# Prompt masks added on VectorE in one operation with the queries' factor and the maximum, probabilities weighed on VectorE head by head

## What is computed

```python
# DSA: the indexer scores keys, the best k_sel are kept, softmax over these
score = einsum('qh,qhs->qs', wi, relu(einsum('qhd,sd->qhs', qi, ki) * D_IDX ** -0.5))
_, sel = top_k(where(key_pos <= pos, score, -inf), k_sel)        # 64 of 256 for the prompt
logits = einsum('qngd,qknd->qngk', qa, ka[sel]) * HEAD_DIM ** -0.5
p = softmax(where(sel <= pos, logits, -inf));  oA = einsum('qngk,qknd->qngd', p, va[sel])
# MoBA: the block of 256 keys that holds the query, causal
p = softmax(where(causal, qb . kb * HEAD_DIM ** -0.5, -inf));    oB = p . vb
x += (sigmoid(gA) * (oA @ w_up_a) + sigmoid(gB) * (oB @ w_up_b)) @ w_out
```

## Time and profile before

| | us |
|---|---|
| runs, median of 3 (lowest, highest) | 639.16 (638.4, 639.34) |
| the profiled execution | 638.18 |
| its span, first to last instruction | 636.6 |
| PE busy | 628.3 (99%) |
| VectorE busy | 408.9 (64%) |
| ScalarE busy | 298.7 (47%) |
| POOL busy | 154.6 (24%) |

### The profile page before, as it was taken

How to read it: one execution, slowest core, us unless ns; L and a number is a source line. 1 busy time by engine, 2 the same in 40 slices (tenths; PEclk the granted TensorE clock), 3 DMA queues, 4 the chain that set the end, 5 groups by cost and what they waited for, 6 DMA issues and landing times.

```text
span 636.6 us, 13030 instructions
## 1 busy us (share of the span) xinstructions
PE 628.3 (99%) x4822; PEld 608.7 (96%) x4822; DVE 408.9 (64%) x671; ACT 298.7 (47%) x480; POOL 154.6 (24%) x211
## 2 busy tenths in 40 slices
PE   8999999999999999999899999999999999999998
PEld 6999999999999999889789899999999999999998
DVE  5765656565555568599888739867565656574441
ACT  7644444444343355545554657454434444443330
POOL 1477776000011216466603100260000000000000
PEclk9999999999999999999999999999999999999999
DMA  8777676535554556633232314545555554555530
GB/s 323 273 223 241 198 241 200 188 129 184 177 164 153 186 157 202 204 125 121 70 132 72 128 68 154 178 132 167 164 158 173 150 180 150 172 153 196 173 106 20
DMA packets 34907, 104.79 MB, mean 165 GB/s; under 512 B 6065, under 2 KB 8753, under 8 KB 34865
## 3 DMA queue, kind: packets, MB, share of 16 engines
q1 hardware_dynamic: 30432, 97.98, 46.6%
q0 software_dynamic: 3616, 4.73, 2.6%
q10 hardware_dynamic: 816, 1.51, 0.6%
HBM read 100.21 MB, written 1.70 MB: 160 GB/s over the span
## 4 chain that ended last, share of the span: by engine, by line
PE 86%; DVE 3%; DMA 2%; POOL 2%; SPq 2%; ACT 2%; issue 1%; ACTq 0%; POOLq 0%
PE ps L1189 27%; PE ps L1191 26%; PE ps L1190 26%; SPq L486 1%; DVE wlo L862 1%; PE ps L1321 1%; DMA x<-in_x 1%; PE ps L1394 1%; PE ps L1353 1%; PE ps L1384 1%; PE ps L1305 1%; ACT whi L627 1%; PE ps L1213 0%; DVE tmp L1102 0%; DMA kv<-kv 0%
## 5 line engine op out<-in xcount | busy, mean ns | idle before, releaser
L862 DVE TENSOR_TENSOR wlo<-raw,whi 128x1024 fp32r<-128x1024 f32 (+2 forms) x180 | 220.2, 1227 | 124.3 <-ACT whi L627 123.9
L1189 PE MATMUL ps<-nhi,whi 128*128 128x288 f32 (+1 forms) x944 | 283.4, 300 | 0.4 <-DVE kv L1092 0.2
L1190 PE MATMUL ps<-nlo,whi 128*128 128x288 f32 (+1 forms) x944 | 278.6, 295 | 0.0
L1191 PE MATMUL ps<-nhi,wlo 128*128 128x288 f32 (+1 forms) x944 | 277.7, 294 | 0.0
L627 ACT ACTIVATE whi<-raw 128x1024 fp32r<-128x1024 f32 (+2 forms) x180 | 181.3, 1030 | 126.9 <-PE ps L1191 114.1
L1189 PEld LDWEIGHTS ps<-nhi,whi 128*128 128x128 f32 (+1 forms) x944 | 176.5, 187 | 5.4 <-issue 3.0
L1191 PEld LDWEIGHTS ps<-nhi,wlo 128*128 128x128 f32 (+1 forms) x944 | 177.4, 188 | 0.0
L1190 PEld LDWEIGHTS ps<-nlo,whi 128*128 128x128 f32 (+1 forms) x944 | 176.9, 187 | 0.3
L1189 PE MATMUL ps<-hhi,whi 128*128 128x288 f32 x336 | 99.5, 296 | 0.0
L1190 PE MATMUL ps<-hlo,whi 128*128 128x288 f32 x336 | 99.2, 295 | 0.0
L1191 PE MATMUL ps<-hhi,wlo 128*128 128x288 f32 x336 | 98.8, 294 | 0.0
(11 more groups left out here) (187 smaller groups left out, 681.0 us busy)
## 6 DMA issues: line engine op xcount, KB each, us to landing
raw<-in_weights SPq DMA_DIRECT2D x164, 512.0 KB, 3.4
raw<-in_weights SPq DMA_DIRECT2D x16, 384.0 KB, 3.6
raw<-in_weights SPq DMA_DIRECT2D x4, 256.0 KB, 5.0
kt<-in_cache_kidx_a POOLq DMA_DIRECT2D x32, 32.0 KB, 2.8
kt<-in_cache_k_b POOLq DMA_DIRECT2D x16, 64.0 KB, 3.0
kt<-in_cache_k_a POOLq DMA_DIRECT2D x32, 32.0 KB, 3.0
vb_pg<-in_cache_v_b POOLq DMA_DIRECT2D x16, 64.0 KB, 3.3
cst<-in_constants ACTq DMA_DIRECT2D x1, 948.0 KB, 8.0
```

The costliest lines, as they stand in the source:

```text
L862: nc.vector.tensor_tensor(wlo[:, v % NU, 0:nk, 0:w], raw[:, v % NR, 0:nk, 0:w], whi[:, v % NU, 0:nk, 0:w].bitcast(F32), ALU.subtract).then ...
L1189: nc.tensor.matmul(out[0:w, 0:N], h, hi, start=start and i == 0, stop=False)
L1190: nc.tensor.matmul(out[0:w, 0:N], h, lo, start=False, stop=False)
L1191: ins = nc.tensor.matmul(out[0:w, 0:N], l, hi, start=False, stop=stop and done is not False and i == len(ks) - 1)
```

## The change

For prompt steps the mask matmuls go. VectorE takes each head's logits out of PSUM in one operation, `tensor_tensor_reduce`: logits plus mask, times the negated factor (`rq_neg`, new, made once for each kind at steps 8 and 16), written to `probs` in SBUF, and the minimum of it to `nmax`, which is the negated maximum of the logits. ScalarE takes its exponentials from there with a scale of -1, and no longer from PSUM. The masks are the float32 constants for MoBA and, for DSA, `acc1` and `acc0`, into which the search now writes its result. Sample steps keep their mask matmuls and their two operations.

The weighing moves from POOL to VectorE, behind each step's reciprocal, one operation per head (two, four, or one for samples), in place.

Waits: VectorE's first operation of a step now waits until the transposes of the step two before have read the buffer, and until a DSA mask is there; it waits for its own reciprocals. PE's next logits wait for the maximum (`max_done`) instead of the exponential where the step before was a prompt step. Two casts to bfloat16 at the start of the kernel go.

```diff
--- before.py
+++ after.py
@@ -279,8 +279,6 @@
...
         cst = new("cst", [P, C_ALL])
-        idb = new("idb", [P, P], BF16)
-        causalb = new("causalb", [P, 2 * P], BF16)
         gains = new("gains", [P, GAIN_ROWS])
...
         tmp = new("tmp", [P, 2, 1, N])
@@ -301,8 +299,6 @@
...
         best = new("best", [P, 8])
-        sel1 = new("sel1", [P, 2 * P], BF16)
-        sel0 = new("sel0", [P, P], BF16)
         sel_s = new("sel_s", [NS_TOK, NK_S], BF16)
...
         nmax = new("nmax", [P, 4 * N_STEPS])
@@ -311,6 +307,7 @@
...
         rq = new("rq", [P, 2, 3 * HEADS])
+        rq_neg = new("rq_neg", [P, 2, 2 * HEADS])
         rsel = new("rsel", [P, 2, HEADS])
...
@@ -363,8 +360,8 @@
...
-        (logits_done, max_raw, max_done, soft_done, rinv_ready, probs_ready, probsT_done, probsT_ready) = [sem(s) for s in
-            "logits_done max_raw max_done soft_done rinv_ready probs_ready probsT_done probsT_ready".split()]
+        (logits_done, max_done, soft_done, rinv_ready, probs_ready, probsT_done, probsT_ready) = [sem(s) for s in
+            "logits_done max_done soft_done rinv_ready probs_ready probsT_done probsT_ready".split()]
...
@@ -429,7 +426,11 @@
...
             step = head_of(kind, 1, 0) - head_of(kind, 0, 0)
-            return rq[:, kind - 1, c0:c0 + step * (len(blocks) - 1) + 1:step]
+            return rq_neg[:, kind - 1, c0:c0 + step * (len(blocks) - 1) + 1:step]
+
+        def prompt_mask(kind, form):
+            return ((c_(C_CAUSAL, 2 * P) if kind == MOBA else acc1[:]) if form == 1
+                    else (c_(C_CAUSAL + P, P) if kind == MOBA else acc0[:]))
...
@@ -566,20 +567,7 @@
...
-            def weigh(m):
-
-                kind, form, i = step_kind(m)
-                nh, w = {1: (2, 2 * P), 0: (4, P), 2: (1, NK_S)}[form]
-                pool.wait_ge(rinv_ready, m - 7)
-                pool.wait_ge(soft_done, m + 1)
-                pv = probs[:, m % 2, 0:nh * w].rearrange("p (h k) -> p h k", h=nh)
-                r = rinv[:, 4 * m:4 * m + nh].unsqueeze(2).to_broadcast([P, nh, w])
-                nc.gpsimd.tensor_tensor(pv, pv, r, ALU.mult).then_inc(probs_ready, 1)
-
             for u in range(U_END):
-                for m in STEPS_OF_SLOT.get(u, []):
-                    if 8 <= m:
-                        weigh(m)
                 if u - ROT_DELAY in ROTATED:
...
                     z = zloc[u - ROT_DELAY]
@@ -753,9 +741,11 @@
...
                     for h in range(nh):
-                        ins = nc.scalar.activation(probs[:, m % 2, h * w:(h + 1) * w], ps[m % 2][:, h * w:(h + 1) * w],
-                                                   ACT.Exp, bias=nmax[:, 4 * m + h:4 * m + h + 1], scale=q_scales(m)[:, h:h + 1],
-                                                   accum_out=rsum[:, 4 * m + h:4 * m + h + 1])
+                        ins = nc.scalar.activation(probs[:, m % 2, h * w:(h + 1) * w],
+                                                       ps[m % 2][:, 0:w] if form == 2 else probs[:, m % 2, h * w:(h + 1) * w],
+                                                       ACT.Exp, bias=nmax[:, 4 * m + h:4 * m + h + 1],
+                                                       scale=q_scales(m) if form == 2 else -1.0,
+                                                       accum_out=rsum[:, 4 * m + h:4 * m + h + 1])
                     ins.then_inc(soft_done, 1)
...
             def outputs_hi(m):
@@ -903,8 +893,6 @@
...
             dve.wait_ge(consts_in, 16)
-            nc.vector.tensor_copy(idb[:], c_(C_ID, P)).then_inc(masks_ready, 1)
-            nc.vector.tensor_copy(causalb[:], c_(C_CAUSAL, 2 * P)).then_inc(masks_ready, 1)
...
@@ -981,8 +969,8 @@
...
-            searches = ((acc1, TOPK_PROMPT // 8, sel1, c_(C_CAUSAL, 2 * P), 0),
-                        (acc0, TOPK_PROMPT // 8, sel0, c_(C_CAUSAL + P, P), 0),
+            searches = ((acc1, TOPK_PROMPT // 8, acc1, c_(C_CAUSAL, 2 * P), 0),
+                        (acc0, TOPK_PROMPT // 8, acc0, c_(C_CAUSAL + P, P), 0),
                         (acc_s, -(-TOPK_SAMPLE // 8), sel_s, c_(C_MASKS, NK_S, NS_TOK), TOPK_SAMPLE % 8))
...
             def search_step(c):
@@ -1006,14 +994,24 @@
...
                     nh, w = {1: (2, 2 * P), 0: (4, P), 2: (1, NK_S)}[form]
-                    dve.wait_ge(logits_done, m + 1)
-                    nc.vector.tensor_reduce(nmax[:, 4 * m:4 * m + nh], ps[m % 2][:, 0:nh * w].rearrange("p (h k) -> p h k", h=nh),
-                                            AX, ALU.max, negate=True).then_inc(max_raw, 1)
-                    dve.wait_ge(max_raw, m - 7)
                     if m == 8 or m == 16:
                         dve.wait_ge(rq_ready, 2 * kind)
-                    nc.vector.tensor_tensor(nmax[:, 4 * m:4 * m + nh], nmax[:, 4 * m:4 * m + nh], q_scales(m), ALU.mult)\
-                        .then_inc(max_done, 1)
+                        link(nc.vector.tensor_scalar(rq_neg[:, kind - 1, :], rq[:, kind - 1, 0:2 * HEADS], -1.0, None, ALU.mult))
+                    dve.wait_ge(logits_done, m + 1)
+                    if form == 2:
+                        link(nc.vector.tensor_reduce(nmax[:, 4 * m:4 * m + 1], ps[m % 2][:, 0:w], AX, ALU.max, negate=True))
+                        nc.vector.tensor_tensor(nmax[:, 4 * m:4 * m + 1], nmax[:, 4 * m:4 * m + 1], q_scales(m), ALU.mult)\
+                            .then_inc(max_done, 1)
+                    else:
+                        if kind == DSA and i == 0:
+                            dve.wait_ge(sel_ready, 2 - form)
+                        if m >= 10:
+                            dve.wait_ge(probsT_done, m - 9)
+                        for h in range(nh):
+                            ins = nc.vector.tensor_tensor_reduce(
+                                probs[:, m % 2, h * w:(h + 1) * w], ps[m % 2][:, h * w:(h + 1) * w], prompt_mask(kind, form),
+                                q_scales(m)[:, h:h + 1], 3.0e38, ALU.add, ALU.min, nmax[:, 4 * m + h:4 * m + h + 1])
+                        ins.then_inc(max_done, 1)
                 if m == 8:
...
                     nc.vector.tensor_tensor(acc_s[:], ps[3][0:NS_TOK, 0:NK_S], c_(C_MASKS, NK_S, NS_TOK), ALU.add)\
@@ -1039,9 +1037,14 @@
...
                 if 8 <= m < N_STEPS:
-                    nh = {1: 2, 0: 4, 2: 1}[step_kind(m)[1]]
+                    nh, w = {1: (2, 2 * P), 0: (4, P), 2: (1, NK_S)}[step_kind(m)[1]]
                     dve.wait_ge(soft_done, m + 1)
                     nc.vector.reciprocal(rinv[:, 4 * m:4 * m + nh], rsum[:, 4 * m:4 * m + nh]).then_inc(rinv_ready, 1)
+                    dve.wait_ge(rinv_ready, m - 7)
+                    for h in range(nh):
+                        pv = probs[:, m % 2, h * w:(h + 1) * w]
+                        ins = nc.vector.tensor_scalar(pv, pv, rinv[:, 4 * m + h:4 * m + h + 1], None, ALU.mult)
+                    ins.then_inc(probs_ready, 1)
...
@@ -1275,8 +1278,10 @@
...
                 banks = (ps[0], ps[1])
-                if m:
+                if 0 < m <= 8 or m in (16, 24):
                     pe.wait_ge(soft_done, m)
+                elif m:
+                    pe.wait_ge(max_done, m - 8)
                 if m == 0:
...
                 if i == 0 and form == 1:
@@ -1286,9 +1291,9 @@
...
                 if m == 8:
-                    pe.wait_ge(masks_ready, 5)
-                if kind == DSA and i == 0:
-                    pe.wait_ge(sel_ready, {1: 1, 0: 2, 2: 3}[form])
+                    pe.wait_ge(masks_ready, 3)
+                if kind == DSA and form == 2:
+                    pe.wait_ge(sel_ready, 3)
                 if m == 0:
...
                 if m == 16:
@@ -1309,19 +1314,12 @@
...
                     nh = len(blocks)
-                    if kind != IDX:
-                        mask = ((causalb[:] if kind == MOBA else sel1[:]) if form == 1
-                                else (causalb[:, P:2 * P] if kind == MOBA else sel0[:]))
-                        for bank in banks:
-                            nc.tensor.matmul(bank[:, :].rearrange("p (h k) -> p h k", h=nh), idb[:],
-                                             mask.unsqueeze(1).to_broadcast([P, nh, w]), start=True, stop=False)
                     for j, b in enumerate(blocks):
...
                                                    Q_OF[kind][rows_, b, form * P:(form + 1) * P],
-                                                   k_new[rows_, 0:w], start=kind == IDX,
-                                                   stop=kind == IDX or j == nh - 1)
+                                                   k_new[rows_, 0:w], start=True, stop=True)
                             if j == nh - 1:
...
```

## The result

The kernel after takes 635.41 us (median of 7 runs, 634.72 to 636.26), the kernel before, measured with it, 638.5 us. The ratio is 0.994 (95% interval 0.9926 to 0.9953): 3.1 us by the medians, 3.8 us (3.0 to 4.7) by the ratio, where 1.15 was forecast. The profiled execution took 636.13 us, 634.5 of them span.

A forecast was written before the change was run, and what follows sets the result against it. PE was taken to bound the end, VectorE having no room where probabilities are weighed late. PE could give 5.2 us, but VectorE's added work left 1.15 at steps 20 and 21: 639.16 - 1.15 = 638.0 us, range 634.8 to 641.4.

The forecast's parts named there:

- PE's share: On PE: 12 mask matmuls gone, 2.9 us, and the wait for POOL's weighing, 2.3 us; 5.2 us earlier at most.
- Price of the masked maximum: On VectorE, start to next start: 0.34 us for 128 and 0.47 for 256 elements, including 0.08 for the read-out.
- ScalarE's read-out: ScalarE's row, 0.09 us from its start to the next exponential's, taken as evidence for 0.08 more per masked maximum.
- Weighing, reciprocals: On VectorE: weighings 0.20 and 0.27 us apart for 128 and 256 elements; each reciprocal, now waited for, 0.20 instead of 0.12.
- The hold by POOL: Steps 10 and 11: POOL's power operation holds VectorE's first weighing until 303.96; without it both weighings end 0.95 us earlier.
- VectorE has no slack from step 12 to step 21: VectorE has no slack up to steps 20 and 21, so its added work delays step 21's weighing to 359.9.
- The three places: PE's transposes at steps 10/11, 12/13 and 20/21: gains 1.6, 0.95 and 1.15 us, with 1 to 2 us waits each.
- Edits at nothing: Logits starting after the maximum, and VectorE's new waits, were costed at nothing.
- (a): Rival: VectorE keeps up, with no read-out cost and no hold; gain 4.7 us, 634.5; chance 0.15 (beyond 3 us).
- (b): Rival: VectorE becomes the bound and the kernel slower, 640.6 to 641.2, or 644 with both upper ends; chance 0.29.
- turning point: On VectorE: 0.036 us more for each of 32 masked maxima turns the forecast gain to nothing.
- (c): Rival: the change doesn't act; the masks' 2.9 us go into VectorE's later waits; gain 0 to 0.5, 638.9; chance 0.16.

The follow-up runs named there:

- masks alone: Kernel after with the weighing put back on POOL in one operation, so only the masks move: ratio 0.998 to the kernel before.
- all three edits: Kernel after with POOL's power operation behind the weighing of steps 8 to 11, search steps parted, maximum handed over head by head: 634.44 us, ratio 0.9925.
- the search parted: Kernel after with VectorE's two search steps of each slot parted, one ahead of the weighing and one behind it: ratio 0.9935 to the kernel before.

## Why the prediction was off

The direction was right, and the time lies in the range, near its lower end; the forecast was 2.6 us too slow. Of that, 0.7 us is the kernel before, measured at 638.5 and not 639.16; a gain of 1.15 us was forecast, and the stretch gives 3.37. By its steps:

- **PE's share.** A mask pair was worth 0.42 to 0.54 us in the shift between the two timelines, 2.7 in all for 2.9. Of the 2.3 us behind POOL, 0.82 stay as waits for VectorE; 1.6 was forecast.
- **Price of the masked maximum: the term that was mis-sized.** 0.34 and 0.47 us were taken, 0.271 (311.34 to 313.51, eight of them) and 0.405 (300.00 to 301.63, four) measured. The lower end of the bound, 0.26 and 0.39, was nearly right, and the choice of ScalarE's read-out as the nearest row was wrong: VectorE's has a row too, 0.08 us long, but nothing waits behind it. 0.065 us times 32 is 2.1 us. The Trainium skill's two instructions ("VectorE: DVE Perf Modes", "Two Vector instructions with no wait between them") are there in the trace as two rows; they cost no second turn.
- What 2.1 us on VectorE are worth: in the forecast's sum VectorE has no lead, so there they count in full, and the measured price alone turns 1.15 into about 3.2 us. In the kernel itself 2.2 us more cost 1.2 to 1.3, since VectorE is 0.77 us ahead of PE at step 21. So by the runs this term accounts for a little over half of the 2.2 us between 1.15 and 3.37. The rest is about the 1.1 us by which the forecast had VectorE's other work between steps 12 and 21 too long (below); no run parts the two.
- **Weighing, reciprocals.** 0.20 and 0.27 us apart and 0.20 a reciprocal, as priced (four of 128 columns take 0.79 us from 356.92 to 357.71).
- **The hold by POOL.** 0.95 us was forecast on the first weighing; 0.41 and 0.56 came on both, and they vanish when POOL's operation is moved. The size was right, the picture (nothing starts until POOL is done) not: of a weighing's two operations one is longer, 0.77 and 0.87 us for 0.35, the other is not, and step 10 is weighed at 304.7, before POOL's operation ends at 305.17.
- **VectorE has no slack from step 12 to step 21: this held, but its work was shorter than forecast.** From the masks of step 12 (311.34) until step 21 is weighed (357.71) VectorE waits for no other engine. From the masks of step 12 to those of 16, 18 and 20 and to step 21 weighed, 20.25, 11.5, 10.65 and 6.7 us were worked out; 19.4, 10.8, 10.17 and 6.0 passed. Without the read-outs (0.55, 0.27, 0.27, 0.55) some 1.1 us is left over. POOL now does nothing from 310 to 362 us, but the splits aren't where it lies: the nine up to the masks of step 20 took 1.214 us in the mean for 1.314, 0.9 us in all, and I had put back 0.8. One candidate, an estimate: the busy times of the earlier trace rows hold 12 waits of VectorE between 310 and 353 us, and an operation ahead of a wait counts there with its full length, 0.08 us more than its distance, 1.0 us in all. No run tried that, so this cause stays open.
- **The three places**, gains counted from the first matmul of step 8: steps 10 and 11 2.0 for the forecast's 1.6, 12 and 13 2.06 for 0.95, 20 and 21 3.37 for 1.15. Two of the three waits were there, with 0.82 and 0.24 us instead of 1 to 2; the third was not.
- **Edits at nothing.** PE has no wait at the logits, and the exponentials out of SBUF were cheaper, not dearer: 0.39 us apart for 128 columns where 0.44 to 0.45 was the price; whether by the place or by the scale, now a constant, isn't parted. The negated factors took 0.17 us at step 16, but 0.77 at step 8 beside POOL's rotation.
- **Rivals.** (a), 634.5, had the right price and the wrong reason for the other half, since the hold is real. (b)'s turning point was 0.036 us a maximum above the price taken; the kernel that stood 0.11 us above the measured 0.27 and 0.41, so about 0.045 above that price, gained nothing clear of noise by the ratio (0.9993, 0.9979 to 1.0007), but 1.0 us at full clock, so the turning point itself isn't shown. (c) falls: the masks' time came through.
- The median moves more than a single trace where clocks differ: in 17 of 50 executions of the kernel before, beside the experiments, the mean clock over the span was 0.997; in none of 7 of the kernel after.

## What to carry to other kernels

Where a queue is near its bound, the price of each repeated operation decides, so take start-to-start distances of the same engine, and when a row of another engine is the nearest, keep the forecast in the middle of both ends. Before work is moved from a slow engine to a busy one, look at what stands ahead of it in the slow engine's queue and what runs beside it: here moving one POOL operation behind the weighing was worth 1.6 us in the kernel before, and with the change it gave the fastest kernel measured here. A saving on the bound engine that lies ahead of a wait only lengthens that wait.

## What was not expected of the hardware

- A wait can cost more than itself: after a stretch with PE busy 1.59 of 4 us the granted clock averaged 0.58 for the next 4 us, and 1.5 us more were lost (masks alone). Behind the 1.96 us of the profiled kernel before it stayed at 1.00. Executions at 0.997 occur in the kernel with all three edits too, 2 of 6, where its profile shows no wait; where the clock fell in those stays open.
- Beside POOL's power operation VectorE's masked maxima, which read PSUM, and its searches ran at their usual length (0.48 and 0.42 us), while the weighings, from SBUF to SBUF, took nearly twice theirs. The form alone doesn't explain this. The power operation is two operations in the trace, 2.92 us on 128x16 and then 1.62 on 32x8; in the kernel after, those maxima and searches lie beside the first (300.67 to 303.59), and step 10's weighing beside the second. In the kernel with the search parted step 10 is weighed beside the first and isn't stretched; the second starts at 302.86, with the weighing of step 11. Why the second holds VectorE and the first does not stays open.

```profile
299.99 4.50 POOL L595 TENSOR_TENSOR rq<-qms,eps_col 128x16 f32<-128x16 f32 x2
302.13 0.62 DVE L1046 TENSOR_SCALAR probs<-probs,rinv 128x256 f32<-128x256 f32 x2
302.86 1.18 DVE L1046 TENSOR_SCALAR probs<-probs,rinv 128x256 f32<-128x256 f32 x2
```
